# Attention and pooling between half pieces of the pool and value projections, head pairs on two row tiles, one scaling for all heads

## What is computed

```python
h = modulate(rmsnorm(x, norm_mix_g[l]), sh_m, sc_m)
q, k, v, f_logit, u = jnp.split(jnp.matmul(h, w_in[l]), split_pts, axis=-1)
log_f = jax.nn.log_sigmoid(f_logit + b_fgate[l])
# logit[t,s] = q_t.k_s/sqrt(dh) + F[t] - F[s], F = cumsum(log_f), causal
attn_out = forgetting_attention(q, k, v, log_f)
# trailing mean over 2, 4, 8, 16 tokens minus the token, a 128x128 map per group, a scale
pool_out = multiscale_pool(u, w_pool[l], pool_scale[l])
mix = jnp.matmul(jnp.concatenate([attn_out, pool_out], axis=-1), w_out[l])
x = x + gt_m[:, None, :] * mix
```

## Time and profile before

| | us |
|---|---|
| median of three runs (lowest to highest) | 1328.21 (1326.38 to 1331.26) |
| the profiled execution: its time | 1314.67 |
| its span, first to last instruction | 1312.8 |
| mean granted TensorE clock in it | 0.935 |

### The profile page before, as it was taken

One profiled execution on the slowest core, in us unless ns is written; L12 is line 12 of the kernel. 1 busy time (PEld: TensorE's weight loads), 2 busy tenths in 40 slices (PEclk: granted clock), 3 DMA queues, 4 the chain that ended last, 5 costly groups with the idle time before them and its releaser, 6 DMA issues.

```text
span 1312.8 us, 22891 instructions
## 1 busy us (share of the span) xinstructions
PE 1203.0 (92%) x9779; PEld 994.3 (76%) x9779; DVE 561.6 (43%) x875; ACT 470.5 (36%) x594; POOL 493.0 (38%) x112
## 2 busy tenths in 40 slices
PE   6999999999787798998999999989689599999995
PEld 5898799999676787997788998887457466666663
DVE  2243211010475664424377878943551613222223
ACT  5444445344533223231544344525021322222222
POOL 4878757878605544020534435627110000000000
PEclk9999999999988989999999999889558599999998
DMA  9655555555503320001399798825105179999970
GB/s 362 213 168 195 176 173 174 190 183 192 191 3 128 105 73 4 3 16 53 117 341 334 282 328 310 285 97 178 46 4 222 82 296 404 423 412 420 413 319 33
DMA packets 99124, 260.87 MB, mean 199 GB/s; under 512 B 6368, under 2 KB 61024, under 8 KB 83184
## 3 DMA queue, kind: packets, MB, share of 16 engines
q1 hardware_dynamic: 93728, 249.78, 51.5%
q10 hardware_dynamic: 5328, 10.09, 2.3%
HBM read 258.80 MB, written 1.05 MB: 198 GB/s over the span
## 4 chain that ended last, share of the span: by engine, by line
PE 48%; issue 24%; POOL 19%; DVE 7%; ACT 2%; DMA 0%; POOLq 0%; DVEq 0%; ACTq 0%
POOL wlo L526 19%; PE ps L2378 9%; PE ps L1719 5%; PE ps L1720 5%; PE ps L1721 5%; PE ps L2405 4%; PE ps L2333 3%; PE ps L2041 1%; PE ps L2050 1%; PE ps L2351 1%; PE ps L2353 1%; PE ps L2054 1%; PE ps L1778 1%; PE ps L2274 1%; PE ps L2277 1%
## 5 line engine op out<-in xcount | busy, mean ns | idle before, releaser
L526 POOL TENSOR_TENSOR wlo<-raw,whi 128x2048 fp32r<-128x2048 f32 x99 | 470.1, 4763 | 477.0 <-ACT whi L574 477.0
L1719 PE MATMUL ps<-Hh,whi 128*128 128x256 f32 x832 | 240.9, 290 | 8.9 <-POOL wlo L526 4.1
L574 ACT ACTIVATE whi<-raw 128x2048 fp32r<-128x2048 f32 x116 | 220.2, 1909 | 64.4 <-DMA raw<-in_ffn_w 33.2
L1720 PE MATMUL ps<-Hl,whi 128*128 128x256 f32 x832 | 238.1, 286 | 0.0
L1721 PE MATMUL ps<-Hh,wlo 128*128 128x256 f32 x832 | 237.9, 286 | 0.0
L1719 PEld LDWEIGHTS ps<-Hh,whi 128*128 128x128 f32 x832 | 161.9, 195 | 14.7 <-POOL wlo L526 6.2
L1720 PEld LDWEIGHTS ps<-Hl,whi 128*128 128x128 f32 x832 | 162.4, 195 | 0.6 <-issue 0.2
L1721 PEld LDWEIGHTS ps<-Hh,wlo 128*128 128x128 f32 x832 | 162.2, 195 | 0.0
L2378 PE MATMUL ps<-w_e,arena 128*64 128x256 f32 x1024 | 114.0, 381 | 0.0
L2378 PEld LDWEIGHTS ps<-w_e,arena 128*64 128x64 f32 x1024 | 72.1, 137 | 37.1 <-issue 0.4
L1719 PE MATMUL ps<-whi,Fh 128*128 128x512 f32 x256 | 99.9, 390 | 0.0
(11 more groups left out here) (370 smaller groups left out, 1957.6 us busy)
## 6 DMA issues: line engine op xcount, KB each, us to landing
raw<-in_ffn_w SPq DMA_DIRECT2D x64, 1024.0 KB, 5.4
w_e<-in_w_expert_gate SPq DMA_DIRECT2D x32, 1024.0 KB, 7.3
w_e<-in_w_expert_up SPq DMA_DIRECT2D x32, 1024.0 KB, 11.1
w_e<-in_w_expert_down SPq DMA_DIRECT2D x32, 1024.0 KB, 10.6
arena<-in_w_ada SPq DMA_DIRECT2D x24, 1024.0 KB, 11.2
raw<-in_sgu_w_in SPq DMA_DIRECT2D x16, 1024.0 KB, 7.0
raw<-in_rwkv_w_rkv SPq DMA_DIRECT2D x12, 1024.0 KB, 4.8
raw<-in_sgu_w_out SPq DMA_DIRECT2D x8, 1024.0 KB, 4.9
```

Source lines behind the costliest of these rows:

```text
L526: pool.tensor_tensor(wlo[n % RING][:, :], raw[n % RING][:, :], whi[n % RING][:, :].bitcast(F32), ALU.subtract).then_inc(lo_done, 1)
L574: act.activation(whi[n % RING][:, :], raw[n % RING][:, :], ACT.Copy).then_inc(hi_done, 1)
L1719: pe.matmul(o, sh, mh, start=start, stop=False, skip_group_check=True)
L1720: pe.matmul(o, sh, ml, start=False, stop=False, skip_group_check=True)
```

## The change

On TensorE the order becomes: q and k pieces with the cumulative sum ahead of the last; then u (now c = 4, 5) and v (c = 6, 7) cut into halves by token tile, and between the halves the scores of a head pair, the transposes of a pair and the pool products; the first output pieces (now those of the pool's features first) between pool maps, weighted values and output transposes. `scores(p)` takes two heads: even heads on partitions 0 to 63, odd heads on 64 to 127, each head one PSUM bank, into which q.k and F[t] - F[s] are both summed. The exponentials are read from PSUM and not scaled; the weighted values are computed with tokens on the partitions, scaled once for all heads of a token tile, and transposed back by eight transposes. The mask is added in PSUM. ScalarE makes the pool's high part, VectorE the low part in one instruction; `prob` and `probT` have places of their own, for four and for all eight heads.

The diff, cut (removed lines stand in the functions above, most are left out here; indentation is shortened by four):

```diff
+rows = np.zeros((P, 2 + AH // 2))
+for odd in range(2):
+    base = HD * odd
+    rows[base + AH:base + 2 * AH, 0] = 1.0
+    rows[base:base + AH, 1] = 1.0
+    for j in range(AH // 2):
+        h = 2 * j + odd
+        rows[base + h, 2 + j] = rows[base + AH + h, 2 + j] = 1.0
...
+FR = HD + 2 * AH
...
+    f_at = 11 * SLOT
+    lf2 = arena[:, f_at:f_at + TT * 2 * FR].rearrange("p (t n) -> p t n", t=TT)
+    f_tmp = arena[:, f_at + 320:f_at + 336]
+    f_a = arena[0:FR, f_at + 384:f_at + 640]
+    f_b = arena[0:FR, f_at + 640:f_at + 896]
+    f_bh = tiles(slot(4)[:, 0:4 * SEQ], 4)[0:FR]
+    prob_at = CST["strict_lower"]
+    def prob(h):
+        if h // 2 % 2 == 0:
+            return slot(8)[:, 384 * (h % 2):384 * (h % 2 + 1)]
+        return cst[:, prob_at + 384 * (h % 2):prob_at + 384 * (h % 2 + 1)]
+    def probT(h):
+        place, n = (slot(0), h) if h < 5 else (slot(9), h - 5) if h < 7 else (slot(4)[:, 1024:SLOT], 0)
+        return place[:, 384 * n:384 * (n + 1)]
+    pdiff = slot(4)[:, 1408:1920].rearrange("p (b n) -> p b n", b=2)
+    att_max, att_sum = gst[:, 0:2 * AH], gst[:, 2 * AH:4 * AH].rearrange("p (t h) -> p t h", t=TT)
+    att_out = tiles(slot(5)[:, 0:1024], TT)
...
-                at = 512 * (c // 2) + (AH if c >= 6 else 0)
+                at = 3 * 512 + AH if c < 6 else 2 * 512
                 load(FIRST["in2"] + c, w[:, 4 * (c % 2):4 * (c % 2) + 4, at:at + 512], k=4)
...
-            load(FIRST["out2"] + c, w[:, 2 * c:2 * c + 2, :], k=2)
+            k = (2 * c + KT // 2) % KT
+            load(FIRST["out2"] + c, w[:, k:k + 2, :], k=2)
...
                     act.wait_ge(sem("f_negabs"), 1)
                     act.activation(fl, fl, ACT.Exp).then_inc(sem("f_ln"), 1)
                     act.wait_ge(sem("f_ln"), 1)
                     act.activation(fl, fl, ACT.Ln, bias=1.0).then_inc(sem("f_ln"), 1)
...
+            def exponentials(p):
+                for h in (2 * p, 2 * p + 1):
+                    act.wait_ge(sem("att_max"), h + 1)
+                    for t, at in ((0, slice(0, P)), (1, slice(P, 3 * P))):
+                        ins = act.activation(prob(h)[:, at], ps[:, 2 * (p % 2) + h % 2, at], ACT.Exp,
+                                             bias=att_max[:, 2 * h + t:2 * h + t + 1],
+                                             accum_out=att_sum[:, t, h:h + 1])
+                    ins.then_inc(sem("att_exp"), 1)
+            def token_copies(dst, first):
+                for t in range(TT):
+                    act.activation(dst[:, t, :], ps[:, first + t, :], ACT.Copy).then_inc(sem("in2_copied"), 1)
+            def pool_high(g):
+                act.wait_ge(sem("pmix_mm"), g + 1)
+                act.activation(C2hT[:, 4 + g, :], ps[:, 6 + g % 2, SEQ:2 * SEQ], ACT.Copy, scale=colv("pool_scale", g)
+                               ).then_inc(sem("c2_hi"), 1)
+            exponentials(0)
+            hi(IN + 7)
+            exponentials(1)
+            act.wait_ge(used, IN + 6)
+            token_copies(utm, 6)
+            exponentials(2)
+            hi(OUT)
+            exponentials(3)
+            hi(OUT + 1)
+            pool_high(0)
+            pool_high(1)
+            act.wait_ge(used, IN + 8)
+            token_copies(vtm, 4)
+            pool_high(2)
+            pool_high(3)
+            hi(OUT + 2)
+            hi(OUT + 3)
+            for j in range(2):
+                act.wait_ge(sem("att_tp"), j + 1)
+                act.activation(C2h[:, 512 * j:512 * (j + 1)], ps[:, 6 + j, :], ACT.Copy).then_inc(sem("c2_hi"), 1)
...
+            z = ps[:, 3, 0:16].rearrange("p (t n) -> p t n", t=TT)
+            e = f_tmp.rearrange("p (t n) -> p t n", t=TT)
             dve.wait_ge(sem("small_in"), 48)
+            do(dve.memset(lf2, 0.0))
...
+            for odd in range(2):
+                at = HD * odd
+                do(dve.tensor_tensor(lf2[:, :, at:at + AH], z, e, ALU.subtract))
+                at = FR + HD * odd + AH
+                ins = dve.scalar_tensor_tensor(lf2[:, :, at:at + AH], z, -1.0, e, ALU.mult, ALU.add)
+                if odd == 0:
+                    do(ins)
+            settle()
+            ins.then_inc(sem("f_log"), 1)
             dve.wait_ge(sem("F_mm"), 1)
+            do(dve.tensor_scalar(f_a, ps[0:FR, 3, 0:SEQ], f_cols[0:FR, 0:1], None, ALU.add))
+            do(dve.tensor_scalar(f_b, ps[0:FR, 2, 0:SEQ], f_cols[0:FR, 1:2], None, ALU.add))
+            settle()
+            for j in range(AH // 2):
+                ins = dve.tensor_scalar(f_bh[:, j, :], f_b, f_cols[0:FR, 2 + j:3 + j], None, ALU.mult)
...
+            def maxima(p):
+                for h in (2 * p, 2 * p + 1):
+                    score = ps[:, 2 * (p % 2) + h % 2, 0:3 * P]
+                    dve.wait_ge(sem("score_mm"), p + 1)
+                    do(dve.tensor_tensor(score, score, causal, ALU.add))
+                    settle()
+                    do(dve.tensor_reduce(att_max[:, 2 * h:2 * h + 1], score[:, 0:P], AX.X, ALU.max, negate=True))
+                    settle()
+                    dve.tensor_reduce(att_max[:, 2 * h + 1:2 * h + 2], score[:, P:3 * P], AX.X, ALU.max, negate=True
+                                      ).then_inc(sem("att_max"), 1)
+            def transposed(p):
+                dve.wait_ge(sem("probT_mm"), p + 1)
+                for h in (2 * p, 2 * p + 1):
+                    ins = dve.tensor_copy(probT(h), ps[:, 2 * (p % 2) + h % 2, 0:3 * P])
+                    if h % 2 == 0:
+                        do(ins)
+                ins.then_inc(sem("probT"), 1)
+            def difference(g):
                 dve.wait_ge(sem("pool_mm"), g + 1)
                 if g >= 2:
                     dve.wait_ge(sem("pmix_mm"), g - 1)
+                dve.tensor_copy(pdiff[:, g % 2, :], ps[:, 6 + g % 2, 0:SEQ]).then_inc(sem("pdiff"), 1)
+            def pool_low(g):
+                dve.wait_ge(sem("c2_hi"), g + 1)
+                dve.scalar_tensor_tensor(C2lT[:, 4 + g, :], ps[:, 6 + g % 2, SEQ:2 * SEQ], colv("pool_scale", g),
+                                         C2hT[:, 4 + g, :].bitcast(F32), ALU.mult, ALU.subtract
+                                         ).then_inc(sem("c2_lo"), 1)
+            settle()
+            maxima(0)
+            maxima(1)
+            transposed(0)
+            maxima(2)
+            transposed(1)
+            maxima(3)
+            transposed(2)
+            difference(0)
+            difference(1)
+            transposed(3)
+            pool_low(0)
+            pool_low(1)
+            difference(2)
+            difference(3)
+            pool_low(2)
+            pool_low(3)
+            dve.wait_ge(sem("att_exp"), AH)
+            do(dve.reciprocal(att_sum, att_sum))
+            settle()
+            for t in range(TT):
+                dve.wait_ge(sem("av_mm"), t + 1)
+                dve.tensor_tensor(att_out[:, t, :].rearrange("p (h s) -> p h s", h=AH),
+                                  ps[:, 4 + t, :].rearrange("p (h s) -> p h s", h=AH),
+                                  att_sum[:, t, :].unsqueeze(2).to_broadcast([P, AH, HD]), ALU.mult
+                                  ).then_inc(sem("att_scaled"), 1)
+            for j in range(2):
+                dve.wait_ge(sem("c2_hi"), 4 + j + 1)
+                dve.tensor_tensor(C2l[:, 512 * j:512 * (j + 1)], ps[:, 6 + j, :], C2h[:, 512 * j:512 * (j + 1)].bitcast(F32),
+                                  ALU.subtract).then_inc(sem("c2_lo"), 1)
...
+            def scores(p):
+                if p >= 2:
+                    pe.wait_ge(sem("probT"), p - 1)
+                pe.wait_ge(sem("in2_copied"), 3 if p < 2 else 4)
+                blocks = ((slice(0, P), 0, P), (slice(P, 3 * P), 1, SEQ))
+                for o, t, s_ in blocks:
+                    tok = slice(P * t, P * (t + 1))
+                    for odd in range(2):
+                        f = slice(HD * odd, HD * (odd + 1))
+                        pe.matmul(ps[:, 2 * (p % 2) + odd, o], qT[f, p, tok], kT[f, p, 0:s_], start=o.start == 0,
+                                  stop=False, skip_group_check=True)
+                for o, t, s_ in blocks:
+                    tok = slice(P * t, P * (t + 1))
+                    for odd in range(2):
+                        f = slice(HD * odd, HD * odd + 2 * AH)
+                        ins = pe.matmul(ps[:, 2 * (p % 2) + odd, o], f_a[f, tok], f_bh[f, p, 0:s_], start=False,
+                                        stop=True, skip_group_check=True)
+                ins.then_inc(sem("score_mm"), 1)
+            def prob_transposes(p):
+                pe.wait_ge(sem("att_exp"), 2 * p + 2)
+                for h in (2 * p, 2 * p + 1):
+                    for b in range(3):
+                        ins = pe.transpose(ps[:, 2 * (p % 2) + h % 2, P * b:P * (b + 1)], prob(h)[:, P * b:P * (b + 1)],
+                                           ident)
+                ins.then_inc(sem("probT_mm"), 1)
+            def pool_mean(g):
+                if g >= 2:
```

(78 more changed lines are left out.)

190 lines of the change are left out of this document (23 added, 167 removed).

## The result

The changed kernel takes 1277.21 us (median of 4 runs, 1271.10 to 1279.18); the kernel before, in the same comparison, 1329.04 us. The ratio is 0.9625 (95% interval 0.9582 to 0.9667). The forecast was 1286.2 us in a range of 1276 to 1305: the direction and the range held, and the gain is 52 us where 42 were forecast. The profiled execution took 1275.34 us, with a span of 1273.3 us and a mean granted clock of 0.951.

What follows compares the result with a forecast made beforehand. Taken as the bound: the mixer's 117.5 us stretch, its attention loop at half clock with TensorE waiting. New TensorE terms sum to 71.3; less 3.4 clock and 1 waits, gain about 42: 1328.2 - 42 = 1286.2 us, range 1276 to 1305.

Steps and rivals of the forecast that it cites:

- the case of a larger gain: Whole kernel: no clock fall and scores at the lower bound, or a median closer to the profiled time; chance 0.04.
- the two falls: Mixer's new order on TensorE: two drops of the granted clock, 1.7 us each, 3.4 us charged.
- Scores: Attention score products on TensorE: 2.1 us a head pair, 8.4 us for four; bounds 6.4 and 12.6.
- Rival C: Score products: row tiles do not overlap, scores 12.6 us, gain 38, time 1290; chance counted within the forecast's 0.66.
- Changes of height: TensorE entering and leaving row tiles between dense pieces: four times 0.4 us, 1.6 us charged.
- Waits: TensorE's stalls: 0.9 us at the first scores for f_bh behind GpSimd, plus 1 us for small waits.
- The covers: Half pieces and other scores hide VectorE's and ScalarE's chain: 4.5 us chain under 7.5 us; failures would cost 8 to 16.
- Rival A: Attention: VectorE and ScalarE chain tighter, or clock low for a third; gain 22 to 35, time 1293 to 1306; chance 0.22.
- rival D: Expert stage: DMA-bound, it gives the gain back; time near 1328; chance 0.03.
- present 39 us: Between mixer and first expert: gated_add, norm and router stay the same 39 us; a later start would show the forecast wrong.
- Rival B: Rewritten stretch: TensorE's clock stays at 1.2 GHz; 140.9 us, 23 more than before, time 1352; chance 0.05.
- The time ahead of it hardly changes: Kernel ahead of the rewritten 117.5 us mixer stretch: its time was claimed to stay nearly the same.

Runs made afterwards that it cites:

- the serial runs: Variants of the changed kernel with attention in one block, nothing laid between the half pieces; 1288.71 us for the first, 1287.58 with scaling per head, 1305.37 with the pool first.
- the ladder: Changed kernel undone part by part (placement, single scaling, pool in the gaps, paired heads), back to the kernel before; intervals 73.7, 86.9, 93.2, 104.4, 111.8, 123.3 us.
- the serial kernel: Changed kernel with nothing laid between the half pieces: u and v pieces, then pool and attention, then output pieces; 1288.71 us, ratio 0.9713, interval 86.85 us.

## Why the prediction was right, and where 10 us were missing

The direction, the mechanism and the range held, the size less so. The measured 1277.2 us lies below the 1280 to 1292 that the prediction took for the forecast with a chance of 0.66, and only 1.2 us inside the range; it is the case of a larger gain that got 0.04. Both reasons named for that case came true: no clock fall, and scores near their lower bound. That the number is still inside the range is in part luck, as nearly all terms were off to the same side.

The working gave 71.3 us from the fourth q/k copy, or 77.1 with the last key piece of 5.8, and 81.5 with the 3.4 for the clock and 1 for small waits. The interval measured 73.74. The 7.8 us between, term by term:

- *Clock, 3.4 us.* The step of the two falls failed. The clock is 1.00 in all windows from the third copy on, through the 5.3 us of 64-column weighted values too. I had taken f_gate's stretch, 3.6 us of 8-column products, for the pattern, and that was the wrong row; why the clock fell there and not here is not shown. The 1.7 us a fall were my estimate and have no row of their own.
- *Scores, 1.6 us.* 1.71 us a pair, not 2.1. I let weight loads pace them at 0.114 us each. The run with one head at a time shows that four instructions of one head need the same 0.85 us as eight of two: the second head's loads are hidden, and one head's products with the change of height behind them are the price. Rival C, without overlap, had 12.6 us for four pairs, 3.15 each; that run gave 3.4.
- *Changes of height, 0.8 us.* The piece's last matmul starts 0.32 us ahead of a pair, and the first one behind it 0.33 ahead of its successor, where 0.23 is the rule: 0.2 us a pair for going in and out, 0.8 for four in place of 1.6.
- *Waits, 1.2 us.* Of 0.9 for `f_bh` and 1 for the rest, only the first came, with 0.65. Its mechanism, VectorE's products held by GpSimd's subtraction, was right, as the read from PSUM shows. (That L1447 ran while GpSimd was busy is so too, though the earlier trace rows does not show it: GpSimd's instruction there runs from 917.90 to 922.40.)
- *The other small terms*, 1.1 us together, were each a little high: transposes 0.66 a pair (2.6, not 3.1), pool 5.2 for 5.4, cumulative sum 1.74 for 1.9, output transposes 0.87 for 1.0, weighted values 5.3 for 5.5.

That is 8.1; 0.3 went the other way.

The covers that the prediction drew up for VectorE and ScalarE held, and the run with three maxima shows the slack behind them: 1.2 us a pair cost nothing. Rival A fell with TensorE's one wait and the clock of 1.00, rival D with the 302.8 us behind the interval against 304.2. (The "present 39 us" to the first expert was read short; it is 41.5 before and 39.8 after, and both values occur among the variants.) Rival B didn't occur, but the serial runs show that its mechanism is real where no pieces stand between: 15 us at 0.50 in the batched form, 44 with the pool taken out, 52 before. "The time ahead of it hardly changes" held for the kernel, not for single executions.

Of the gain of 51.8 us the interval has 49.5 and the time behind it 1.4. What is left is under 1 us and too small to tell. Profile against profile the gain is only 39.3 us, as the profile of before was an execution 13.5 us below the median, with the full clock at 500 to 540; to take the gain off the median was right. Against its repetition the spans differ by 54.6 us, and the medians by 51.8.

What the prediction didn't ask is what each part is worth. By the ladder the placement, which the title names first, carries 13.1 of 49.5 us, and about half of that is the clock. The order of undoing matters: the scaling per head costs 6.3 us in the serial kernel, 3.5 of them by a collision with GpSimd, and nothing between the pieces. The 2.2 us of half pieces stand against the placed kernel and are not a step of their own.

## What to carry to other kernels

The block of small products cost twice here: by its waits and by the lower clock that it and its neighbour then ran at; look at the granted clock of the stretch before counting instructions. Batching such a block (heads side by side on row tiles, one scaling, the pool's gaps filled) and laying it between dense pieces overlap in what they save, so judge each with the other in place; here, with the batching done, the placement was worth 13 us. When a step's price is read from one run, look whether VectorE's work from SBUF to SBUF was held by GpSimd in it. Once TensorE has no waits left, an engine's slack can be told by adding work to it, and a term of TensorE's sum should be taken from the nearest row at the same clock.
